# Products of the next weights while TensorE waits: attentions, norms and stick-breaking of a two-block transformer

## The reference, cut to what matters

```python
# first block, per layer: modulated norm, mixer, gated norm of its result, conv-FFN, gated norm
xm = modulate(h, g_pre_m, sh_m, sc_m)
y = even_mixer(...)   # layer 0: gMLP half + neighbourhood attention with a bias table and context keys
y = odd_mixer(...)    # layer 1: q, k normed per head and rotated, 16 heads over 768 keys
h = h + gt_m * rms_norm(y, g_post_m)
h = h + gt_f * rms_norm(conv_ffn(modulate(h, ...)), g_post_f)
# second block, per layer: SwiGLU, a mixer of three attentions, SwiGLU
x = x + 0.5 * g1 * swiglu(h, w_ffn1_gu[l], w_ffn1_down[l])
o_a = mla_attention(qa, ka, va)              # latent, causal, 6 heads, 64 + 32 rotated columns
o_b = swa_attention(qb, kb, vb, ...)         # window of 128, relative bias, sinks, 6 heads
o_c = stick_breaking_attention(qc, kc, vc)   # 4 heads, log-sigmoid and a reversed cumulative sum
x = x + g2 * (mix(rms_norm_2(o_a), rms_norm_2(o_b), rms_norm_2(o_c)) @ w_out[l])
x = x + 0.5 * g3 * swiglu(h, w_ffn2_gu[l], w_ffn2_down[l])
```

## Time and profile before

| | us |
|---|---|
| median of 3 runs | 4225.49 |
| profiled execution | 4221.91 |
| its span | 4220.1 |
| TensorE busy | 3874.7 |
| DVE busy | 1993.7 |
| POOL busy | 1524.3 |
| ACT busy | 1400.6 |

### The profile page before, as it was taken

How to read it: one execution, slowest core, us unless ns; L and a number is a source line. 1 busy time by engine, 2 the same in 40 slices (tenths; PEclk the granted TensorE clock), 3 DMA queues, 4 the chain that set the end, 5 groups by cost and what they waited for, 6 DMA issues and landing times. The chain is left out here.

```text
span 4220.1 us, 51879 instructions
## 1 busy us (share of the span) xinstructions
PE 3874.7 (92%) x19016; PEld 3022.0 (72%) x19016; DVE 1993.7 (47%) x3503; ACT 1400.6 (33%) x2168; POOL 1524.3 (36%) x738
## 2 busy tenths in 40 slices
PE   6978899999788889999999779899999998879999
PEld 5866688888566668876887643688878876437887
DVE  3786866443646676654454854322232231452222
ACT  3244322222326443333223253322232233433222
POOL 1330143444130135553544310455545443104454
PEclk9989999999989999999999877999999999779999
DMA  7611144432110136653663210233323332102232
GB/s 241 187 36 30 44 140 131 148 105 64 32 38 1 38 107 220 214 167 129 226 226 119 65 40 1 60 95 94 96 83 95 94 86 67 34 1 79 91 97 78
DMA packets 460357, 411.40 MB, mean 97 GB/s; under 512 B 28080, under 2 KB 405296, under 8 KB 460208
## 3 DMA queue, kind: packets, MB, share of 16 engines
q1 hardware_dynamic: 457759, 408.11, 31.3%
q10 hardware_dynamic: 2448, 1.32, 0.1%
HBM read 405.71 MB, written 7.60 MB: 98 GB/s over the span
## 5 line engine op out<-in xcount | busy, mean ns | idle before, releaser
L212 POOL TENSOR_TENSOR s_wlo<-s_raw,s_whi 128x1024 fp32r<-128x1024 f32 x490 | 1181.2, 2418 | 2112.5 <-ACT s_whi L204 2112.0
L226 PE MATMUL psum<-s_xhi,s_whi 128*128 128x512 f32 x3264 | 1230.3, 377 | 52.7 <-DVE s_t L391 19.8
L227 PE MATMUL psum<-s_xlo,s_whi 128*128 128x512 f32 x3264 | 1222.9, 375 | 0.0
L228 PE MATMUL psum<-s_xhi,s_wlo 128*128 128x512 f32 x3264 | 1218.0, 373 | 0.0
L204 ACT ACTIVATE s_whi<-s_raw 128x1024 fp32r<-128x1024 f32 x490 | 510.6, 1057 | 1827.4 <-PE psum L228 1822.6
L226 PEld LDWEIGHTS psum<-s_xhi,s_whi 128*128 128x128 f32 x3264 | 617.0, 189 | 175.0 <-issue 53.5
L227 PEld LDWEIGHTS psum<-s_xlo,s_whi 128*128 128x128 f32 x3264 | 616.8, 189 | 112.3 <-issue 4.6
L228 PEld LDWEIGHTS psum<-s_xhi,s_wlo 128*128 128x128 f32 x3264 | 616.0, 189 | 111.8
L226 PE MATMUL psum<-s_ahi,s_whi 128*128 128x512 f32 x1232 | 476.6, 387 | 10.8 <-DVE s_y L1128 7.1
L228 PE MATMUL psum<-s_ahi,s_wlo 128*128 128x512 f32 x1232 | 469.7, 381 | 0.0
L227 PE MATMUL psum<-s_alo,s_whi 128*128 128x512 f32 x1232 | 469.5, 381 | 0.0
(11 more groups left out here) (263 smaller groups left out, 4174.8 us busy)
## 6 DMA issues: line engine op xcount, KB each, us to landing
s_ada_raw<-w_ada SPq DMA_DIRECT2D x224, 512.0 KB, 3.8
s_raw<-w_gu SPq DMA_DIRECT2D x176, 512.0 KB, 3.8
s_raw<-w_up SPq DMA_DIRECT2D x88, 512.0 KB, 4.8
s_raw<-w_dn SPq DMA_DIRECT2D x88, 512.0 KB, 3.5
s_raw<-w_down SPq DMA_DIRECT2D x44, 512.0 KB, 4.4
s_raw<-w_in SPq DMA_DIRECT2D x30, 512.0 KB, 3.9
s_raw<-w_in_ab SPq DMA_DIRECT2D x20, 512.0 KB, 6.3
s_area<-w_first SPq DMA_DIRECT2D x16, 512.0 KB, 11.8
```

The lines of the kernel that those rows point to most:

```text
L212: pool.tensor_tensor(K.wlo[:, c % HL, 0:a * b], K.raw[:, c % RAW, 0:a * b], K.whi[:, c % HL, 0:a * b].bitcast(F32), ALU.subtract).then_inc ...
L226: pe.matmul(out, lh, rh, start=first, stop=False)
L227: pe.matmul(out, lh, rl, start=False, stop=False)
L228: return pe.matmul(out, ll, rh, start=False, stop=last)
```

## The change

A new method `hold` waits until the high half of the next chunk is there and multiplies its first 128 columns with its first 512, n times, into a bank that the phase doesn't use (7, or 5 in the norm). Nobody reads the result; the bank is written anew by its next user. It is called in seven places, ahead of waits of TensorE.

```diff
+    def hold(self, pe, n, bank=7):
+        K, c = self.K, self.c_next
+        pe.wait_ge(K.sem["w_hi"], c + 1)
+        for _ in range(n):
+            pe.matmul(K.pf[:, bank * BANK:(bank + 1) * BANK], K.whi[:, c % HL, 0:P], K.whi[:, c % HL, 0:BANK], start=True, stop=True)
@@ Norm.pe, after the eight sums of squares n
+            if n == 0 and self.sums == 2:
+                self.hold(e, 25 if T == T0 else 32, 5)
@@ Attn.pe
         for s in range(min(self.ns, n)):
             scores(s)
+        self.hold(e, 6 if self.pairs else 12 if self.wide and not self.bias else 22)
@@ HeadNorm.__init__
             up_chunk(K, w, col, self.base["out_ready"] + self.place["tile", i] + 1, n)
+        self.c_next = len(K.chunks)
@@ HeadNorm.pe, ahead of the rotations of the last two tiles
+                if j >= len(self.tiles) - 2:
+                    self.hold(e, 8 if j == len(self.tiles) - 2 else 16)
                 e.wait_ge(self.sem["qn_ready"], self.at("qn_ready", j + 1))
@@ Stick.pe
+        e.wait_ge(self.sem["bias_ready"], self.at("bias_ready"))
+        self.hold(e, 24)
         self.drained(e)
...
         for kt in range(4):
+            if kt == 2:
+                self.hold(e, 18)
             logits(0, kt)
@@ MlaNorm.pe
+        self.hold(e, 10)
         e.wait_ge(self.sem["mla_r"], self.at("mla_r", 1))
```

## The result

The changed kernel takes 4203.48 us (median of 5 runs, 4198.77 to 4207.60) against 4225.49 (4222.82 to 4228.16): ratio 0.9949, 95% interval 0.9934 to 0.9964. It is 22 us faster; I had forecast 40. Its profiled execution took 4206.46 us with a span of 4204.7, and a mean granted clock of 0.967 (0.951 before). Worked out as in the prediction, that is 278 us at the lower clock (2 x 0.033 x 4204.7) instead of 414: 136 us less at 1.2 GHz, for a gain of 22.

The account below looks back on a forecast made before the run. TensorE, busy 92% of the span but partly at half clock, was taken to bound the kernel. Terms -0.4 + 0 + 2.2 + 3.6 + 4 + 1 + 30 = 40.4 us off 4221.9 gave 4181.5, named 4185; range 4170 to 4215.

Parts of the forecast that it names:

- where the money is: Latent attention stage of both layers, TensorE-bound at 1.2 GHz: 15.0 us saved a layer, 30.0 for two.
- first case: All as forecast, the clock staying high in the latent stages: 4185 us, own range 4175 to 4195, chance 47%.
- first rival: Clock falls in the latent norm's ten spread products, is lifted later by the six: 26 us gain, 4199, chance 27%.
- (a): Latent stage, ten spread products from the row sums: 13.70 us become about 7.2 at the high clock, 6.5 saved a layer.
- (b): Latent attention, first three scores: 7 us become 3.7, transposes 1.0 earlier a layer; the six added products fit the gap.
- (c): Latent attention, first transposes to four steps on: 19.5 us become 11.9 at the high clock, 7.5 saved a layer.
- Stick-breaking and windows: Stick-breaking's logits and window attention, two layers: 4 us saved in stick-breaking for both, 1 in the windows.
- Head norms and odd attention: Faster rotations, projection, scores and transposes: 2.2 us saved at the keys' head norm, 3.6 at the queries' with odd attention.
- Norms: Four runs of added products; DVE sets the rounds behind them, so 0 and -0.4 us, the overrun in 512-token norms.
- neighbourhood attention: 5.3 us of added products in a 14.4 us wait; the clock falls as before in the idling left: 0.
- first four of the 29 products: Same products already in the kernel: 29 take 8.46 us, read as four at 0.43 us (low clock), the others at 0.24.

Follow-up runs that it names:

- ten_only: The changed kernel with only the ten added products ahead of the latent norm's spread kept, both layers: 4212.36 us, 12.4 faster than the kernel before.
- six_only: The changed kernel with only the six added products behind the latent attention's first scores kept, both layers: 4214.18 us, 8.1 faster than the kernel before.
- again_before: The kernel before, run and profiled once more with no edit: 4223.24 us against 4220.24 in the same job, ratio 1.0004.
- again_after: The changed kernel, run and profiled once more with no edit: 4203.17 us, 21.6 faster than the kernel before.
- without_latent: The changed kernel without its ten and six products in the latent stages, the other 324 kept: 4217.90 us, 6.9 faster than the kernel before.
- heads_stick: The changed kernel with only the added products of head norms, odd layer's attention and stick-breaking kept: 4221.19 us, 1.1 faster than the kernel before.
- norms_windows: The changed kernel with only the added products of norms, neighbourhood and window attentions kept: 4225.82 us, 3.6 slower than the kernel before.

## Why the prediction was right in its direction and half wrong in its size

**What bounds, where the money is: right.** The two latent stages carry the gain, and the medians follow their sum within 5 us in all nine kernels. My first case (47%, 4175 to 4195) did not come; the 4203.48 lies near the 4199 of the first rival (27%).

**(a) Spread products, 6.5 a layer: nearly right, and a matter of place.** At 1.00 they took 7.53 us for my 7.2, and the step to the scores gave 5.5; where the clock fell within them (layer 1, 10.67 us) it gave 3.0, and no edit explains which of the two comes (ten_only). Forecast 13.0 for both, measured 8.5.

**(b) Scores, 1.0 a layer, and the six products at no cost: wrong, the step that failed.** I took the whole stage for one question: it stays high or it doesn't. It fell behind the spread. The scores stayed at 7 us and the six cost 2.9: the first transposes, against the scores' start, came 2.65 us later instead of 1.0 earlier. That is 3.7 us a layer, 7.3 in all.

**(c) Four steps, 7.5: right in its number** (19.5 to 11.7 us), by luck: I had the clock high from the ten on, and it had fallen. What lifted it was the step of the first rival, the six at the low clock. six_only and ten_only show that it is these and not the ten. Behind the four steps the clock fell again for a while, which gave back 0.9 a layer.

**Stick-breaking and windows, 5: 0.1 and 3.2.** The gain of layer 0 is real in its stage (2.2 to 2.4 us in all five profiles that have these products) and given back behind it.

**Head norms and odd attention, 5.8: 3.7 in its place, and not seen in the total.** The keys' head norm (1130 to 1223 us) gains 2.0 to 2.2 in all five profiles that have these products, for my 2.2; the queries' with the first scores (1223 to 1285) gains 1.5 to 1.7, for my 3.6. In the eight other profiles both stretches agree with the kernel before within 0.25. But where the odd attention ends (1422 to 1453) seven of those eight, again_before among them, are 3.2 us shorter than the first profile of the kernel before, and none of the five is; the norm at 1896 is 2.9 shorter in six of the eight and in none of the five. The gain is real where it arises, and something of its size is missing behind it. That the products cause this is likely from such counts and not shown.

**Norms, -0.4; neighbourhood attention, 0: as forecast within what can be told.** The 3.5 us lost in that attention are in again_before too (3.6).

**A row read wrongly.** I had the clock low for the first four of the 29 products of the earlier trace rows. Their starts in the trace are 0.43 us apart from the fourth to the twelfth, and the clock is low from 499.1 to 502.5: eight of them were slow. The 0.43 stands.

Added up, of my 40.4: (a) -4.5, (b) -7.3, the clock behind the four steps -1.7, (c) +0.6, and outside the latent stages 4.9 (22.0 - 17.1) instead of 10.4, -5.5: 22. The 4.9 is a median less the sum of one profile. The profiled executions themselves differ by 15.5 us, so there it is -1.6, and 0.3 in again_after: whether anything outside the latent stages reached the total is not told. The 6.9 us of without_latent speak for it, heads_stick and norms_windows against it. The first rival ("falls in the ten, lifted later", 4199) came nearest: 26 forecast, 22 measured. Only it put the fall into the ten products in both layers; it came behind them in layer 0.

The rule of the Trainium skill (TensorE: Matmul & The Clock Gate, What's actually happening) that I weighed, under 1% of a span at stake, is not contradicted: no version gained more than 22 us, 0.5%. That 9.8% of the span is at 1.2 GHz stands as the trace shows it; taking 136 us of it away brought 22.

## What to carry to other kernels

Fill waits with idle products only where TensorE, busy and at half clock, sets the pace behind them: 32 products there did all that 356 did, within the 5 to 6 us of the intervals. Judge each stage at several places, for a clock that is held up may fall a few microseconds later, and products added inside such a stage can cost more than they bring: one behind every second spread product took the whole gain, six behind the last 2 us a layer. And profile the unchanged kernel twice before a stage table is believed to 3 us, and compare a place over all versions that leave it alone: that told the 3.7 us of the head norms from the 3.2 that come and go behind them, and the place where the clock falls in the spread from an effect of an edit.

## What the runs showed of the hardware that I had not expected

Dense products at the low clock paid for themselves: 2.93 us of them saved 7.6 behind them, in work that had stayed at 0.50 for 41 us of full business without them.

The ten spread products with ten dense ones ahead of them took 7.53 us six times and 10.5 to 10.8 six times: where the clock fell was not settled by the products ahead of it.

A DVE operation of 0.43 us took up to 2.53 beside POOL's split of the weights. The Trainium skill (SBUF — State Buffer, SBUF: two separate sides) says that VectorE and GpSimd share a pair of ports that is locked for a whole instruction; the trace agrees: 2.53 against the 2.48 of one of the two POOL operations (4.95 / 2). The chain of the bias table, with such meetings in every profile, took 69.4 to 69.9 us in the three compared above.
